# A two-layer hybrid encoder: the first two in-projection units by halves of the tokens, with all input tiles kept in SBUF and their squares behind the hi parts

## The chip, the core and the metric

The kernel runs on one core of one Trainium2 chip. The metric is the device time of one execution in microseconds, as the median of several runs. The engines that matter here are TensorE (PE in the profile), ScalarE (ACT), VectorE (DVE), GpSimd (POOL) and SyncE (SP), which only issues DMAs in this kernel.

## What is computed

Two layers over 1024 tokens of width 1024, in float32. Only the beginning of layer 0 is touched:

```python
def rms_norm(x, g, eps=EPS):
    xf = x.astype(jnp.float32)
    y = xf * lax.rsqrt(jnp.mean(xf * xf, axis=-1, keepdims=True) + eps)
    return (y * g.astype(jnp.float32)).astype(x.dtype)
...
h = rms_norm(x, norm_mix[0])
proj = h @ w_in                 # 1024 x 3328 columns: 26 units of 128
gate_b, gate_c, u = jnp.split(proj[..., :1536], 3, axis=-1)
y_a = gate_b * causal_depthwise_conv(gate_c * u, conv_w)
```

Behind it come the RWKV-7 mixer on the other 1792 columns, an output projection and a squared-ReLU MLP, then in layer 1 a sliding-window attention and a second MLP.

## The kernel before

**Layout.** The activations are kept with channels on the partitions and tokens on the free axis, as 8 chunks (k) of 128 channels by 1024 tokens. A float32 product is done as three: each operand is split into a high part in the reduced type fp32r (`h_hi`, `w_hi`, written by ACT) and the rest (`h_lo`, `w_lo`, written by DVE), and PE computes hi times hi, lo times hi and hi times lo. A unit is 128 columns of the weight: for each of 8 chunks three products, each for two halves of 512 tokens, 48 matmuls in all (`product`, L278), accumulated in two PSUM banks. Unit j uses weight slot j % 2 and banks 0 and 1, or 2 and 3.

**Input.** x comes with tokens on the partitions, in 8 tiles of 128 tokens by 1024 channels (512 KB), loaded by DMAs on POOL's queue (L1841) into `XIN`, which holds four; from the fifth on a load waits until the tile before it in that place is transposed and squared. PE transposes a tile by 8 matmuls with the identity (L1947) into two PSUM banks, taking banks 0 and 1 or 2 and 3 in turn, and ACT copies them into the residual `X` (L1901). DVE multiplies by the gain of the norm (L1992), ACT casts to `h_hi` (`x_high`, L1889), DVE subtracts to get `h_lo` (L1999). The products use x times gain without 1/rms, which is applied behind them, when a unit leaves PSUM. For 1/rms ACT squares the token-major tile with a row sum into `SSQ` (L1906), between its copy and its cast.

**1/rms.** ACT takes the root of the sums (L508, behind a table load), DVE the reciprocals (L516). PE spreads them over the partitions by 8 transposes into banks 4 and 5 (`spread` in `norm_between`, L546), inserted in unit 0 ahead of its chunk k = 5. ACT copies them to `RI` (`rms_spread`, L512). DVE's `scale_out` (L557) takes a unit out of PSUM, times `RI`, and frees its banks.

**Order.** PE waits for all eight tiles of `h_lo`, then does units 0 and 1 and 24 more in a loop. SP loads unit u into slot u % 2 once the low part of unit u - 2 is done (`load_unit`, L227). ACT casts it (`split_hi`, L233) once the unit that used the slot is through PE, DVE subtracts (`split_lo`, L237). For the first 12 units DVE's loop in `in_dve` is: low split of unit j + 1, wait for unit j, scale it out; after every third unit the convolution, five more operations (L822 to L831), whose result POOL stores with a DMA (L1844, `ya_spill`). Then `shift` does the token shift of each of the other 14 units.

Of the kernel before, what the change touches and what calls it, by code (L numbers as in the profile page):

```python
# [17 lines left out]
ACT = mybir.ActivationFunctionType  # L18
# [4 lines left out]
P = 128  # L23
D = 1024
S = 1024
KD = D // P
# [62 lines left out]
def hybrid_trunk(nc, x, norm_mix, norm_mlp, mlp_up, mlp_down, w_in_ab, conv_w, shift_mu, w0,  # L89
# [46 lines left out]
    RIV = at("rms_inverse_tokens", [2 * NT], 188.6875)  # L136
    XIN = at("x_in_tile", [4, KD, P], 120)
    VROW = at("vector_rows", [P], 136)

# [33 lines left out]
    with ExitStack() as ctx:  # L173
# [10 lines left out]
        ident_in, const_in, late_in = sem("ident_in"), sem("const_in"), sem("late_const_in")  # L184
        x_in = [sem(f"x_in{j}") for j in range(4)]
        lora_zero, dist_in = sem("lora_pads_zero"), sem("distances_in")
# [604 lines left out]
        def in_act(act):  # L791
            def splits(first, end):
                with act.Fori(first, end) as i:
                    for j in range(2):
                        split_hi(act, 1 - j, i + j, 2 * i + j + 2)

            splits(0, 7)
            act.wait_ge(shift_done, 2 + 2)
            nc.scalar.activation(WA[0:RH, :], WA[0:RH, :], ACT.Tanh).then_inc(lora_act, 1)
            nc.scalar.activation(GL[:, :], GL[:, :], ACT.Sigmoid).then_inc(lora_act, 1)  # L800
            splits(7, 12)
            split_hi(act, 1, 12, 26)

        def in_dve(dve):
# [4 lines left out]
            with dve.Fori(0, 2) as i:  # L809
                for q in range(2):  # L810
                    for r in range(3):
                        j = 3 * q + r
                        split_lo(dve, (j + 1) % 2, 6 * i + j + 1)
                        dve.wait_ge(acc_done, 6 * i + j + 3)
                        dve.wait_ge(conv_done, 2 * i + q + 1)
                        scale_out(dve, (ST0[:, 0:S], ST1[:, 0:S], WA[:, 0:S])[r], j % 2)
                    g = 2 * i + q
                    w = VT[:, bass.ds(V_CW + g, 1)], VT[:, bass.ds(V_CW + 4 + g, 1)], \
# [17 lines left out]
            dve.wait_ge(shift_zero, 2)  # L836
            split_lo(dve, 1, 13)
            dve.wait_ge(gl_free, 5)
# [928 lines left out]
        def x_banks(tile):  # L1767
            return PS[:, 2 * (tile % 2):2 * (tile % 2) + 2, :].rearrange("p b (k n) -> p (b k) n", n=P)

# [60 lines left out]
        def _(pool):  # L1830
# [6 lines left out]
            for tile in range(NT):  # L1837
                if tile >= 4:
                    pool.wait_ge(x_tr, 2 + tile - 3)
                    pool.wait_ge(x_sq, tile - 3)  # L1840
                pool.dma_start(XIN[:, tile % 4], xin[tile]).then_inc(x_in[tile % 4], 16)  # L1841
            for g in range(4):
# [49 lines left out]
        def _(act):  # L1892
# [5 lines left out]
            for tile in range(NT):  # L1898
                cols = slice(tile * P, tile * P + P)
                act.wait_ge(x_tr, tile + 3)  # L1900
                nc.scalar.copy(X[:, :, cols], x_banks(tile)).then_inc(x_ev, 1)  # L1901
                if tile == NT - 1:
                    x_high(act, tile)
                if tile:
                    act.wait_ge(x_sq, tile)
                nc.scalar.activation(ST0[:, 0:S], XIN[:, tile % 4], ACT.Square, accum_out=SSQ[:, tile:tile + 1])\  # L1906
                    .then_inc(x_sq, 1)
                if tile < NT - 1:
                    x_high(act, tile)
                if tile == NT - 3:  # L1910
                    split_hi(act, 0, 0, 1)
            act.wait_ge(eps_set, 2)
# [25 lines left out]
        def _(t):  # L1938
# [3 lines left out]
            t.wait_ge(ident_in, 16)  # L1942
            for tile in range(NT):
                t.wait_ge(x_in[tile % 4], 16 * (tile // 4) + 16)
                t.wait_ge(x_ev, tile + 1)
                for k in range(KD):
                    m = nc.tensor.transpose(x_banks(tile)[:, k], XIN[:, tile % 4, k], ident)  # L1947
                m.then_inc(x_tr, 1)
                if tile == 0:
                    t.wait_ge(const_in, 16 * N_EARLY)  # L1950
                    nc.tensor.transpose(PS[:, 7, 0:V_ROWS], VROW[0:V_ROWS, :], ident[0:V_ROWS, 0:V_ROWS])\
                        .then_inc(vec_t, 1)
            t.wait_ge(h_lo, NT)
            product(t, 0, 0, 0, 0, 8, P, 0, Hh, Hl, between=norm_between(t, "in"))
            product(t, 1, 1, 0, 1, 8, P, 0, Hh, Hl)
            with t.Fori(1, 13) as i:
# [15 lines left out]
        def _(dve):  # L1972
# [8 lines left out]
            dve.wait_ge(vec_t, 1)  # L1981
            nc.vector.tensor_copy(VT[:, 0:V_ROWS], PS[:, 7, 0:V_ROWS]).then_inc(vec_ok, 1)
            dve.wait_ge(vec_ok, 1)
# [3 lines left out]
            for tile in range(NT + 1):  # L1987
                if tile < NT:
                    dve.wait_ge(x_ev, tile + 3)
                    if tile >= 2:  # L1990
                        dve.wait_ge(h_lo, tile - 1)
                    nc.vector.tensor_tensor(GX[tile % 2], X[:, :, tile * P:tile * P + P], vb(V_MIX, KD),  # L1992
                                            ALU.mult).then_inc(x_gain, 1)
                if tile == NT - 1:
                    split_lo(dve, 0, 0)
                if tile:
                    dve.wait_ge(h_hi, tile)
                    cols = slice((tile - 1) * P, tile * P)
                    nc.vector.tensor_tensor(Hl[:, :, cols], GX[(tile - 1) % 2], Hh[:, :, cols].bitcast(F32),  # L1999
                                            ALU.subtract).then_inc(h_lo, 1)  # L2000
            rms_invert(dve, 0)
            in_dve(dve)
# [42 lines left out]
```

## Time and profile before

| | |
|---|---|
| median of three timed runs | 2477.88 us |
| lowest and highest | 2476.68, 2485.06 us |
| the profiled execution's own time | 2479.71 us |
| its span (first to last instruction) | 2477.9 us |
| granted TensorE clock, mean | 0.971 |

The times of the rows below count from the first instruction of the span. Busy time of PE is the modelled time of matmuls, which overlap, so two matmuls that start 0.23 us apart can each be shown as 0.39 long. The granted clock is a share of the full 2.4 GHz.

### The profile page before, as it was taken

Reading aid. Unit: us, or ns where it says so; the run is one execution under the profiler, and the core shown is the slowest. Engines: PE = TensorE matmul, PEld = TensorE weight load, DVE = VectorE, ACT = ScalarE, POOL = GpSimd, SP = SyncE. Lnnn points to the kernel's source line nnn. Section 1 sums busy time; section 2 is a strip of 40 time slices with the busy share of each in tenths; the row PEclk is TensorE's granted clock in tenths of the full one; section 3 lists DMA queues with packets and bytes.
Section 4 is the critical chain, followed back from the end, with each engine's and each line's share of the span. In section 5 each row is a group of like instructions: output and inputs, shape, how many; then the busy total and the mean of one; then the engine's idle time right before and its main releaser. Section 6 shows DMA issues by size and latency. Waiting matters only on the chain.

```text
span 2477.9 us, 41465 instructions
## 1 busy us (share of the span) xinstructions
PE 2352.4 (95%) x16338; PEld 1918.6 (77%) x16338; DVE 1429.0 (58%) x1990; ACT 786.9 (32%) x1258; POOL 424.1 (17%) x405
## 2 busy tenths in 40 slices
PE   6999979999899999999999799787999999999999
PEld 5888867877787888888888688445878888888887
DVE  3444467775427567656765633575265766567655
ACT  5111134543304223322333222464142233223323
POOL 0000011111141102111111600242411121112110
PEclk7999989997999999999999899899999999999999
DMA  3221100000111111111111111000111111111112
GB/s 114 68 82 51 43 9 3 3 4 32 33 49 43 51 58 45 51 51 59 47 46 59 38 52 34 9 1 18 42 43 58 54 42 51 59 51 45 48 60 85
DMA packets 166156, 110.85 MB, mean 45 GB/s; under 512 B 3598, under 2 KB 163684, under 8 KB 166052
## 3 DMA queue, kind: packets, MB, share of 16 engines
q1 hardware_dynamic: 163756, 100.39, 13.5%
q0 software_dynamic: 2240, 8.91, 1.1%
q8 instruction: 83, 1.36, 0.2%
q14 instruction: 21, 0.17, 0.0%
q10 hardware_dynamic: 56, 0.01, 0.0%
HBM read 102.49 MB, written 6.29 MB: 44 GB/s over the span
## 4 chain that ended last, share of the span: by engine, by line
PE 88%; DVE 6%; issue 2%; ACT 2%; POOL 2%; DMA 0%; SPq 0%; DVEq 0%; POOLq 0%; ACTq 0%
PE ps L278 36%; PE ps L383 23%; PE ps L376 13%; PE ps L938 2%; PE ps L960 1%; PE ps L1646 1%; DVE probs L1674 1%; DVE softmax_stats L1679 1%; PE ps L332 1%; PE ps L989 1%; PE ps L1460 1%; POOL stage L488 1%; POOL stage L491 1%; PE ps L1615 1%; PE ps L1120 1%
## 5 line engine op out<-in xcount | busy, mean ns | idle before, releaser
L233 ACT CAST w_hi<-w_raw 128x1024 fp32r<-128x1024 f32 x180 | 189.3, 1052 | 854.0 <-PE ps L278 628.7
L278 PE MATMUL ps<-h_hi,w_hi 128*128 128x512 f32 x1312 | 411.8, 395 | 31.3 <-DVE h_lo L522 17.5
L278 PE MATMUL ps<-h_lo,w_hi 128*128 128x512 f32 x1312 | 408.2, 393 | 0.0
L278 PE MATMUL ps<-h_hi,w_lo 128*128 128x512 f32 x1312 | 407.5, 392 | 0.0
L672 DVE TENSOR_TENSOR residual<-residual,ps 128x512 f32<-128x512 f32 x448 | 299.8, 686 | 165.8 <-PE ps L383 162.1
L278 PEld LDWEIGHTS ps<-h_hi,w_hi 128*128 128x128 f32 x1312 | 246.1, 190 | 85.1 <-issue 13.3
L278 PEld LDWEIGHTS ps<-h_lo,w_hi 128*128 128x128 f32 x1312 | 249.0, 190 | 52.7
L278 PEld LDWEIGHTS ps<-h_hi,w_lo 128*128 128x128 f32 x1312 | 248.7, 190 | 52.4
L237 DVE TENSOR_TENSOR w_lo<-w_raw,w_hi 128x1024 fp32r<-128x1024 f32 x180 | 222.3, 1235 | 33.8 <-ACT w_hi L233 33.7
L640 POOL TENSOR_TENSOR w_sums_raw<-w_raw 128x256 f32<-128x256 f32 x64 | 52.5, 820 | 1076.6 <-DMA w_raw<-in_mlp_down 656.9
L376 PE MATMUL ps<-h_hi,w_hi 128*128 128x512 f32 x512 | 199.2, 389 | 0.0
L376 PE MATMUL ps<-h_lo,w_hi 128*128 128x512 f32 x512 | 199.2, 389 | 0.0
L376 PE MATMUL ps<-h_hi,w_lo 128*128 128x512 f32 x512 | 199.2, 389 | 0.0
L654 DVE SCALAR_TENSOR_TENSOR stage<-ps,rms_inverse 128x1024 f32<-128x1024 f32 x32 | 39.2, 1225 | 213.1 <-PE ps L278 213.1
L383 PE MATMUL ps<-t_hi,w_sums_hi 128*128 128x512 f32 x384 | 150.0, 391 | 0.0
L383 PE MATMUL ps<-t_hi,w_sums_lo 128*128 128x512 f32 x384 | 149.7, 390 | 0.0
L383 PE MATMUL ps<-t_lo,w_sums_hi 128*128 128x512 f32 x384 | 149.6, 390 | 0.0
L580 ACT CAST w_sums_hi<-w_sums_raw 128x1024 fp32r<-128x1024 f32 x64 | 67.1, 1048 | 231.0 <-POOL w_sums_raw L646 231.0
L557 DVE TENSOR_TENSOR stage<-ps,rms_inverse 128x1024 f32<-128x1024 f32 x31 | 38.0, 1225 | 130.0 <-PE ps L278 127.9
L376 PEld LDWEIGHTS ps<-h_hi,w_lo 128*128 128x128 f32 x512 | 96.1, 188 | 19.9
L376 PEld LDWEIGHTS ps<-h_hi,w_hi 128*128 128x128 f32 x512 | 96.1, 188 | 19.9
L376 PEld LDWEIGHTS ps<-h_lo,w_hi 128*128 128x128 f32 x512 | 96.1, 188 | 19.9
(295 smaller groups left out, 3899.3 us busy)
## 6 DMA issues: line engine op xcount, KB each, us to landing
w_raw<-in_mlp_up SPq DMA_DIRECT2D x64, 512.0 KB, 4.0
w_raw<-in_mlp_down SPq DMA_DIRECT2D x64, 512.0 KB, 3.4
w_raw<-in_w_in_ab SPq DMA_DIRECT2D x26, 512.0 KB, 3.8
w_raw<-in_w_qkv SPq DMA_DIRECT2D x10, 512.0 KB, 4.0
x_in_tile<-in_x POOLq DMA_DIRECT2D x8, 512.0 KB, 4.1
w_raw<-in_w_out_ab SPq DMA_DIRECT2D x8, 512.0 KB, 3.7
w_raw<-in_w_o SPq DMA_DIRECT2D x8, 512.0 KB, 3.6
out<-out_chunk SPq DMA_DIRECT2D x8, 512.0 KB, 3.2
```

Source lines behind the costliest of these rows:

```text
L233: nc.scalar.copy(WH[:, slot], WR[:, slot]).then_inc(w_hi, 1)
L237: nc.vector.tensor_tensor(WL[:, slot], WR[:, slot], WH[:, slot].bitcast(F32), ALU.subtract).then_inc(w_lo, 1)
L278: m = nc.tensor.matmul(acc(a_slot, half), ww, xx[:, k, half * HALF:(half + 1) * HALF], start=first, stop=last)
L332: m = nc.tensor.matmul(acc(j, half), ww, xx[:, k, half * HALF:(half + 1) * HALF], start=first, stop=last, skip_group_check=True)
L376: m = nc.tensor.matmul(acc(slot, half), ww, xx[:, k, half * HALF:(half + 1) * HALF], start=first, stop=last)
L383: m = nc.tensor.matmul(PS[:, bank_n, :], ww[:, c], xx[:, c], start=new and c == 0 and ww is wh and xx is bh, stop=c == 1 and ww is wl, ski ...
L557: nc.vector.tensor_tensor(dst, acc2(slot), RI[:, :], ALU.mult).then_inc(acc_free[slot], 1)
L580: nc.scalar.copy(WSH[:, d % 2], WSR[:, d % 2]).then_inc(s_hi, 1)
L640: TT(raw[:, 0], a21, a22, ALU.add).then_inc(w_sum, 1)
L654: return nc.vector.scalar_tensor_tensor(dst, src, 0.0, scale, ALU.max, ALU.mult)
L672: dn_dve.done(TT(xk, xk, PS[:, bank_n, :], ALU.add), step)
L938: m = MM(block_bank(bank_n, 32)[quarter(q), h], left[quarter(q), h], right[quarter(q), h], start=True, stop=True)
```

## The change

- `XIN` holds all 8 tiles, so POOL issues the eight loads with no wait between them; the vector rows' buffer moves behind it.
- The transposes of the input use PSUM banks 4 to 7 instead of 0 to 3, and the transposed vector rows bank 3 instead of 7.
- On ACT the eight squares stand behind the last cast to `h_hi` instead of between copy and cast of each tile. The cast of tile t - 1 stands behind the copy of tile t. The high parts of weights 0 and 1 are made behind the casts of tiles 3 and 5.
- PE does units 0 and 1 by halves of the tokens: unit 0 for tokens 0 to 511, as soon as four tiles of `h_lo` and the first weight are there (tile 7 is transposed inside it, behind its first chunk), unit 1 for the same tokens, then, when all of `h_lo` is there, unit 0 and unit 1 for tokens 512 to 1023. The spread of 1/rms stands inside the last of the four, ahead of its chunk k = 1.
- On DVE the low splits of weights 0 and 1 are done inside the input loop, and in `in_dve` the low split of unit j + 2 stands behind the scale-out of unit j instead of the low split of unit j + 1 ahead of it.

```diff
-    XIN = at("x_in_tile", [4, KD, P], 120)
-    VROW = at("vector_rows", [P], 136)
+    XIN = at("x_in_tile", [NT, KD, P], 120)
+    VROW = at("vector_rows", [P], 152)
...
-            splits(0, 7)
+            split_hi(act, 0, 1, 3)
+            splits(1, 7)
...
                     for r in range(3):
                         j = 3 * q + r
-                        split_lo(dve, (j + 1) % 2, 6 * i + j + 1)
                         dve.wait_ge(acc_done, 6 * i + j + 3)
                         dve.wait_ge(conv_done, 2 * i + q + 1)
                         scale_out(dve, (ST0[:, 0:S], ST1[:, 0:S], WA[:, 0:S])[r], j % 2)
+                        split_lo(dve, j % 2, 6 * i + j + 2)
...
-            split_lo(dve, 1, 13)
             dve.wait_ge(gl_free, 5)
...
         def x_banks(tile):
-            return PS[:, 2 * (tile % 2):2 * (tile % 2) + 2, :].rearrange("p b (k n) -> p (b k) n", n=P)
+            return PS[:, 4 + 2 * (tile % 2):6 + 2 * (tile % 2), :].rearrange("p b (k n) -> p (b k) n", n=P)
...
             for tile in range(NT):
-                if tile >= 4:
-                    pool.wait_ge(x_tr, 2 + tile - 3)
-                    pool.wait_ge(x_sq, tile - 3)
-                pool.dma_start(XIN[:, tile % 4], xin[tile]).then_inc(x_in[tile % 4], 16)
+                pool.dma_start(XIN[:, tile], xin[tile]).then_inc(x_in[tile], 16)
...
                 nc.scalar.copy(X[:, :, cols], x_banks(tile)).then_inc(x_ev, 1)
-                if tile == NT - 1:
-                    x_high(act, tile)
+                if tile:
+                    x_high(act, tile - 1)
+                if tile in (4, 6):
+                    split_hi(act, tile // 2 - 2, 0, 2)
+            x_high(act, NT - 1)
+            for tile in range(NT):
                 if tile:
                     act.wait_ge(x_sq, tile)
-                nc.scalar.activation(ST0[:, 0:S], XIN[:, tile % 4], ACT.Square, accum_out=SSQ[:, tile:tile + 1])\
+                nc.scalar.activation(ST0[:, 0:S], XIN[:, tile], ACT.Square, accum_out=SSQ[:, tile:tile + 1])\
                     .then_inc(x_sq, 1)
-                if tile < NT - 1:
-                    x_high(act, tile)
-                if tile == NT - 3:
-                    split_hi(act, 0, 0, 1)
...
+            def x_transposes(tile):
+                t.wait_ge(x_in[tile], 16)
                 t.wait_ge(x_ev, tile + 1)
                 for k in range(KD):
-                    m = nc.tensor.transpose(x_banks(tile)[:, k], XIN[:, tile % 4, k], ident)
+                    m = nc.tensor.transpose(x_banks(tile)[:, k], XIN[:, tile, k], ident)
                 m.then_inc(x_tr, 1)
...
+            def first_units(j, half, between):
+                for k in range(KD):
+                    if k in between:
+                        between[k]()
+                    w_h, w_l = WH[:, j, k * P:k * P + P], WL[:, j, k * P:k * P + P]
+                    for ww, xx in ((w_h, Hh), (w_h, Hl), (w_l, Hh)):
+                        first, last = k == 0 and ww is w_h and xx is Hh, k == KD - 1 and ww is w_l
+                        m = nc.tensor.matmul(acc(j, half), ww, xx[:, k, half * HALF:(half + 1) * HALF],
+                                             start=first, stop=last)
+                if half:
+                    m.then_inc(acc_done, 1)
+
+            x_transposes(0)
+            t.wait_ge(const_in, 16 * N_EARLY)
+            nc.tensor.transpose(PS[:, 3, 0:V_ROWS], VROW[0:V_ROWS, :], ident[0:V_ROWS, 0:V_ROWS]).then_inc(vec_t, 1)
+            for tile in range(1, NT - 1):
+                x_transposes(tile)
+            t.wait_ge(w_lo, 3)
+            t.wait_ge(h_lo, 4)
+            first_units(0, 0, {1: lambda: x_transposes(NT - 1)})
+            t.wait_ge(w_lo, 4)
+            t.wait_ge(vec_ok, 1)
+            first_units(1, 0, {})
             t.wait_ge(h_lo, NT)
-            product(t, 0, 0, 0, 0, 8, P, 0, Hh, Hl, between=norm_between(t, "in"))
-            product(t, 1, 1, 0, 1, 8, P, 0, Hh, Hl)
+            first_units(0, 1, {})
+            first_units(1, 1, {1: norm_between(t, "in")[5]})
...
-                if tile == NT - 1:
-                    split_lo(dve, 0, 0)
...
+                if tile in (4, 7):
+                    split_lo(dve, tile // 7, tile // 7)
             rms_invert(dve, 0)
```

## Rows read from the trace of the kernel before

**Rows 1.** The page of the kernel before, its part 1: engine, busy us (share of the span), instructions.

```profile
PE 2352.4 (95%) x16338; PEld 1918.6 (77%) x16338; DVE 1429.0 (58%) x1990; ACT 786.9 (32%) x1258; POOL 424.1 (17%) x405
```

**Rows 2.** Waits of PE, 37 to 330 us: us in total, times, longest.

```profile
PE ps L278 <- DVE h_lo L1999: 10.1, 1, 10.1
PE ps L1037 <- ACT prep_t L1161: 4.1, 1, 4.1
```

**Rows 3.** The chain of waits, 0 to 60 us: start, us, what.

```profile
12.76 1.24 DVE stage L1992
14.01 1.05 ACT h_hi L1889
```

**Rows 4.** Timeline, input tiles: start, us, engine, line, operation, out<-in, count, idle before.

```profile
8.79 3.62 PE L1947 MATMUL ps<-constants,x_in_tile 128*128 128x128 f32 x16
...
9.51 1.23 DVE L1992 TENSOR_TENSOR stage<-residual,vectors 128x1024 f32<-128x1024 f32 x1
...
12.62 1.06 ACT L1906 ACTIVATE stage<-x_in_tile 128x1024 f32<-128x1024 f32 x1
...
12.87 1.07 PE L1947 MATMUL ps<-constants,x_in_tile 128*128 128x128 f32 x8 [0.46 <-ACT residual L1901]
13.58 0.19 ACT L1906 ACTIVATION_READ_ACCUMULATOR stage<-x_in_tile 128x1 f32 x1
...
14.96 1.01 ACT L1901 COPY residual<-ps 128x1024 f32<-128x1024 f32 x1
...
16.00 1.23 DVE L1992 TENSOR_TENSOR stage<-residual,vectors 128x1024 f32<-128x1024 f32 x1 [0.89 <-ACT residual L1901]
...
16.11 1.94 PE L1947 MATMUL ps<-constants,x_in_tile 128*128 128x128 f32 x8 [2.18 <-ACT residual L1901]
...
17.15 1.22 DVE L1999 TENSOR_TENSOR h_lo<-stage,h_hi 128x1024 fp32r<-128x1024 f32 x1
```

**Rows 5.** Timeline of DVE alone, 60 to 120 us.

```profile
63.34 1.23 DVE L557 TENSOR_TENSOR stage<-ps,rms_inverse 128x1024 f32<-128x1024 f32 x1 [8.43 <-PE ps L278]
...
74.21 1.23 DVE L557 TENSOR_TENSOR decay_aaa_in<-ps,rms_inverse 128x1024 f32<-128x1024 f32 x1 [8.52 <-PE ps L278]
75.47 1.23 DVE L822 TENSOR_TENSOR stage<-stage,decay_aaa_in 128x1024 f32<-128x1024 f32 x1
```

**Rows 6.** Timeline, from the last square to the end of unit 0.

```profile
36.37 0.19 ACT L1906 ACTIVATION_READ_ACCUMULATOR stage<-x_in_tile 128x1 f32 x1
...
37.88 1.22 PE L278 MATMUL ps<-h_hi,w_hi 128*128 128x512 f32 x2 [10.07 <-DVE h_lo L1999]
...
38.25 0.20 DVE L516 RECIPROCAL rms_inverse_tokens<-rms_inverse_tokens 128x8 f32<-128x8 f32 x1 [0.43 <-ACT rms_inverse_tokens L508]
...
47.27 1.03 PE L546 MATMUL ps<-constants,rms_inverse_tokens 128*128 128x128 f32 x8
...
48.35 1.02 ACT L512 COPY rms_inverse<-ps 128x1024 f32<-128x1024 f32 x1 [10.12 <-PE ps L546]
...
52.55 1.23 DVE L557 TENSOR_TENSOR stage<-ps,rms_inverse 128x1024 f32<-128x1024 f32 x1 [0.98 <-PE ps L278]
```

**Rows 7.** Lines L332 and L278: count, ns min/median/max, first and last start us.

```profile
L332 PE MATMUL ps<-h_hi,w_lo x32: 387/389/628, 634.9 to 676.7; 128*128 128x512 f32 x32
...
L278 PE MATMUL ps<-h_hi,w_lo x318: 389/389/389, 64.0 to 279.1; 128*128 128x512 f32 x159
```

**Rows 8.** Slices, PE alone: from:to, length, PE busy, granted clock, DMA share, GB/s.

```profile
15.00:16.00 1.00, 0.00 (x0) 0.95 0.79 98
...
43.00:44.00 1.00, 1.00 (x5) 0.90 0.00 0
```

**Rows 9.** DMA queues, 5 to 9 us: packets, MB, share; an issue: KB, us to landing.

```profile
q0 software_dynamic: 427, 1.55, 98.5%
q1 hardware_dynamic: 92, 0.04, 3.4%
...
w_raw<-in_w_in_ab SPq DMA_DIRECT2D x1, 512.0 KB, 7.4
```

More of the change, by code:

```diff
@@ L184, in hybrid_trunk @@
         ident_in, const_in, late_in = sem("ident_in"), sem("const_in"), sem("late_const_in")
-        x_in = [sem(f"x_in{j}") for j in range(4)]
+        x_in = [sem(f"x_in{j}") for j in range(NT)]
         lora_zero, dist_in = sem("lora_pads_zero"), sem("distances_in")
@@ L1942, in _ @@
             t.wait_ge(ident_in, 16)
-            for tile in range(NT):
-                t.wait_ge(x_in[tile % 4], 16 * (tile // 4) + 16)
+            def x_transposes(tile):
+                t.wait_ge(x_in[tile], 16)
                 t.wait_ge(x_ev, tile + 1)
                 for k in range(KD):
-                    m = nc.tensor.transpose(x_banks(tile)[:, k], XIN[:, tile % 4, k], ident)
+                    m = nc.tensor.transpose(x_banks(tile)[:, k], XIN[:, tile, k], ident)
                 m.then_inc(x_tr, 1)
[L1949 to L1952, printed above, removed]
+            def first_units(j, half, between):
[20 more added lines that the diff above has]
+            first_units(1, 0, {})
             t.wait_ge(h_lo, NT)
-            product(t, 0, 0, 0, 0, 8, P, 0, Hh, Hl, between=norm_between(t, "in"))
-            product(t, 1, 1, 0, 1, 8, P, 0, Hh, Hl)
+            first_units(0, 1, {})
+            first_units(1, 1, {1: norm_between(t, "in")[5]})
             with t.Fori(1, 13) as i:
@@ L1981, in _ @@
             dve.wait_ge(vec_t, 1)
-            nc.vector.tensor_copy(VT[:, 0:V_ROWS], PS[:, 7, 0:V_ROWS]).then_inc(vec_ok, 1)
+            nc.vector.tensor_copy(VT[:, 0:V_ROWS], PS[:, 3, 0:V_ROWS]).then_inc(vec_ok, 1)
             dve.wait_ge(vec_ok, 1)
```

## The prediction

> **What bounds the kernel now.** First the page [rows 1]: TensorE (PE) is busy for 95% of the span, so almost every microsecond that is not a matmul is a wait of PE, and what matters is where these waits are. The view of waits, for PE alone and from 37 us to the end of the in-projection [rows 2], shows two: 10.1 us before the first product, until the last `h_lo` tile is there, and 4.1 us at the start of the next stage, behind the shifts of the last units. Between them 26 units run with no gap, one each 10.87 us. So the kernel pays for the time to the first product, 37.88 us, and then for PE's work. The chain of waits [rows 3] says what that time is: DVE gain, ACT cast, ACT copy, and round again, one tile of 128 tokens each 3.24 us (gains at 12.76 and 16.00 [rows 3, 4]). The timeline [rows 4] shows why: ACT does four things per tile, copy 1.01, square 1.06 and 0.19, cast 1.05, and they follow one another without a gap. DVE has only two operations of 1.23 and PE 1.07 to 1.94 of transposes.
>
> **When the first product can start after the change.** The squares leave ACT's loop, so a tile costs ACT two instructions, 2.0 us. DVE becomes the slower one: gain(t), then h_lo(t-1), 1.15 from start to start (16.00 to 17.15 [rows 4]), then gain(t+1), which waits for DVE's own h_lo(t-1) to be complete; such a dependent pair is 1.26 from start to start (74.21 to 75.47 [rows 5]). That makes 2.41 us a tile. Gain(0) stays at 9.51 [rows 4]. Tile 1 is transposed in half of the group of 16 (3.62 us from 8.79 [rows 4]), by 10.6, and is copied 10.7 to 11.7; gain(1) 11.75, h_lo(0) 12.9, gain(2) 14.16, gain(4) two tiles on at 18.98, h_lo(3) 20.13, the first weight's low part 21.28, done at 22.50 (a split is the same operation as h_lo, 1.22 [rows 4]). Its high part is made on ACT behind the cast of tile 3 (17.85 to 18.9), by 19.9, inside DVE's time: nothing. Tile 6 is transposed behind the copy of tile 4 (done 17.4), by 19.4. So the half products start at 22.6 instead of 37.88, **15.3 us earlier**.
>
> **What PE does from there.** Units end where DVE's scale-outs start: unit 0 by 52.55, unit 1 by 63.34, unit 2 by 74.21 [rows 5, 6], the later ones 10.87 apart. Now there are four half units of 24 matmuls, as many as two whole units, and one weight load for each matmul in both forms. Another place already works by halves (L332): the median of its matmuls is 389 ns, as is that of L278 in the body of the in-projection [rows 7]. No extra. Added inside is only tile 7's transposes. They last 1.94 at the low clock [rows 4], but lie in a stretch that is low anyway: the clock was low, 1.2 GHz, from the first product to about 43.2 (the granted share is 0.90 in the slice from 43 [rows 8], so a fifth of it at one half), 5.3 us after PE began. I take the same 5.3 us from 22.6 on. Eight transposes at full clock are 1.07, at the low one 1.94, and what they put off from the low stretch runs fast, so they cost **1.0**. The spread of `RI` (1.03 [rows 6]) is in both. Before, two units took 37.88 to 63.34, 25.5 us. After: 22.6 + 25.5 + 1.0 = 49.1, against 63.34.
> The four parts separately: first units 0 half 0 to 31.7 (three matmuls and the transposes to 25.9, then five more at 0.45, twice the 0.2265 that 10.87 / 48 gives for one at the full clock, then 16 at 0.2265), unit 1 half 0 to 37.1, unit 0 half 1 to 42.5, unit 1 half 1 with the spread to 49.0, which agrees with the 49.1 above. Sum: 15.3 - 1.0 = **14.3 us earlier** at unit 2.
>
> **Covers, and what each costs if it goes.** *Second weight:* DVE goes on with gain(5) 22.5, h_lo(4), gain(6) 24.9, h_lo(5), gain(7) 27.3, h_lo(6) 28.4, second low part 29.6 to 30.8, last h_lo to 31.9. PE wants the second weight at 31.7 (0.9 to spare) and the last h_lo at 37.1 (5 to spare). *Squares:* they stand behind the last cast, ACT 29.5 to 38.9 (eight of 1.15, 12.62 to 13.77 [rows 4], and 0.03 for each one's wait on the one before). Table load, root and reciprocal take 1.9 more (36.56 to 38.45 [rows 6]), 40.9. PE wants the reciprocals after the first k of the last half, at 43.2: 2.3 to spare, and beyond that each microsecond costs one. *Scales and unit 2:* the spread now comes after unit 0, so unit 0's scale-out waits for `RI`, ACT's cast of weight 2 stands behind the `RI` copy, and DVE's split behind the scale-out. From the spread's start to the copy 1.08 (47.27 to 48.35 [rows 6]), copy 1.02, scale-out 1.15 to the next start, split 1.22: 4.5 us, ready at 47.7, while PE needs it at 49.0 (21 matmuls and the spread are 5.8). 1.3 to spare, whatever the clock does before it.
> *Low splits in the loop:* split of unit j+2 behind scale-out j is the old order shifted, except that at every third unit it stands ahead of the convolution's five operations instead of behind them. ACT's cast for it runs beside the scale-out, so it delays the convolution by 1.2 us and takes 1.2 from its end; DVE idles 8.5 us before such a unit and PE is never short there [rows 2, 5]. The SP queue's loads of those units are released earlier, not later. The `ya_spill` stores on POOL's queue start 1.2 us later; DVE's scale-out of unit 12 waits for the last of them, and PE needs that bank only a unit later. Nothing.
> *Loads:* POOL issues the last four input tiles at once instead of at 10.7 to 20.8, beside the small vector rows and SP's two weights. In the slice 5 to 9 us the POOL queue had 98.5% of the engines' time and moved 1.55 MB, SP's 3.4% [rows 9], so I let all input go first: eight tiles of 0.52 MB at 0.39 MB/us are 10.8 us, from about 4 to about 15, all before PE's turn at tiles 5 to 7. Weight 0 landed 7.4 after its issue, at 11.8, with four tiles ahead [rows 9]; four tiles more are 5.4 us, so 17.2. It is wanted on ACT at 18.9 and DVE stands still only if it lands after 20.2. Nothing, and if weights share with tiles, sooner.
>
> **The sum.** The profiled execution took 2479.7 with a span of 2477.9; median of the three timed runs 2477.88. The span would be 2463.6, that execution's own time 2465.4, the median **2463.6 us**. Behind unit 2 everything hangs on PE or on chains that start with it, so I carry all 14.3 to the end.
>
> **Clock and transposes.** Tile 3's eight transposes took 1.07 [rows 4], as the spread's eight at full clock, 1.03 [rows 6], and PE had run nothing but transposes; the eight of tile 4, after a pause of 2.2 us, took 1.94 and the granted clock had fallen at 15.9 (a granted share of 0.95 in the slice from 15 [rows 8]). The Trainium skill (TensorE: Matmul & The Clock Gate, Part 4: PE-mode transpose) says that the full clock doesn't engage for transposes. By that rule tile 3 should have been slow; the trace speaks against it.
>
> **Rivals.**
> A. *DVE's loop doesn't speed up* (it stays at a tile each 3.24 us, for a wait that I don't see). Then h_lo(3) ends as before, near 24.9, the split at 26.1, and the gain is 37.88 - 26.1 - 1.0 = 10.8: 2467.1. For it: three engines in turn hand the tile on. Against: the PSUM pairs let ACT copy a tile ahead. 0.07. This is the lower bound of the gain.
> B. *Transposes don't count toward the clock's rise.* The low stretch from 22.6 lasts 1.94 longer, costing half of it: 2464.6. The skill's rule above is of this kind. Against: tile 3. 0.10.
> C. *The clock is still up at 22.6.* It last fell 2.0 us after PE stopped; here the pause is 3 us or more, so it should have fallen, but one fall is thin evidence. Unit 0 half 0 would end at 29.2 and PE would wait for the second weight, 30.8: gain 0.8 more, 2462.8. 0.15.
> D. *The reciprocals are late.* Squares or root take over 2.3 us longer, PE stands at the spread: 1 to 3 us lost, 2465 to 2467. Against: ACT has nothing else to do then. 0.06.
> E. *Absorbed.* A later stage is paced by something that didn't move (a load, DVE's backlog), and the time stays near 2478. For it: the 4.1 us at the stage border. Against: that wait is DVE's shifts of the last unit, which start when PE ends it. 0.04.
> F. *Slower: the first weight starves behind eight input tiles.* Place: ACT's cast of weight 0, with copies 5 to 7 queued behind it. PE then starts 2.3 after the landing; it eats the gain from a landing at 34.5 on, and is slower by over 0.3% from 42. For it: 3.4% of the engines for SP while tiles moved. Against: the tiles are through by 15. 0.02.
> Mine: 0.56.
>
> **Range and chances.** 0.3% of the time, 7.4 us, is about what a measurement of this kernel can tell from no change, so faster means under 2470.4. My case with A to D gives 2462.8 to 2467.1. The timed runs reach from 1.2 below their median to 7.2 above it, and later stages with a changing clock may shift a microsecond or two either way: 2460.0 to 2468.5. Faster 0.94 (mine, A to D), same 0.04 (E), slower 0.02 (F).
>
> **What the changed profile would show.** First half product near 22.6 (over 25: A, or the landing of weight 0); DVE gains 2.4 apart; squares on ACT from about 29.5 to 39; PE's clock low to about 28; no wait of PE at the spread (else D); unit 2 from about 49; every later stage 14 us earlier. The forecast is wrong if PE waits anew between 31 and 49, or if the stages behind don't move with it.

## The result, and the profile after

The changed kernel took 2462.23 us (median of six runs, 2456.04 to 2471.02), the kernel before in the same rounds 2477.28 (2475.13 to 2488.42). The ratio is 0.9922, with a 95% interval of 0.9892 to 0.9951: faster by more than 0.3%. The median lies in the predicted range, 1.4 us from the forecast. The ratio times the 2477.88 shown before is 2458.6, and that lies 1.4 us below the range. Two executions in a slower state, one of each kernel, are left out of the ratios and means of this document; with them the difference of the means given further down, 17.4 us, would be 16.5.

The profiled execution of the changed kernel has a span of 2469.2 us, only 8.7 less than that of before. Its front answers to the prediction within a few tenths. First the timeline of the changed kernel, the first tile's transposes, tiles 2 and 3, the first half product, and what follows to unit 2 (start, us, engine, line, operation):

```profile
5.87 1.94 PE L1944 MATMUL ps<-constants,x_in_tile 128*128 128x128 f32 x8 [5.87 <-DMA x_in_tile<-in_x]
...
14.33 1.23 DVE L2009 TENSOR_TENSOR stage<-residual,vectors 128x1024 f32<-128x1024 f32 x1
15.47 1.22 DVE L2014 TENSOR_TENSOR h_lo<-stage,h_hi 128x1024 fp32r<-128x1024 f32 x1
...
16.79 1.22 DVE L2009 TENSOR_TENSOR stage<-residual,vectors 128x1024 f32<-128x1024 f32 x1
...
17.69 1.06 PE L1944 MATMUL ps<-constants,x_in_tile 128*128 128x128 f32 x8 [0.94 <-ACT residual L1898]
...
22.80 0.80 PE L1954 MATMUL ps<-h_hi,w_hi 128*128 128x512 f32 x1 [4.04 <-DVE w_lo L237]
...
29.80 1.06 ACT L1907 ACTIVATE stage<-x_in_tile 128x1024 f32<-128x1024 f32 x1
...
39.04 0.18 ACT L1907 ACTIVATION_READ_ACCUMULATOR stage<-x_in_tile 128x1 f32 x1
...
40.93 0.20 DVE L516 RECIPROCAL rms_inverse_tokens<-rms_inverse_tokens 128x8 f32<-128x8 f32 x1 [8.71 <-ACT rms_inverse_tokens L508]
...
43.00 1.03 PE L546 MATMUL ps<-constants,rms_inverse_tokens 128*128 128x128 f32 x8
```

```profile
45.48 1.22 DVE L557 TENSOR_TENSOR stage<-ps,rms_inverse 128x1024 f32<-128x1024 f32 x1 [4.34 <-ACT rms_inverse L512]
46.62 1.22 DVE L237 TENSOR_TENSOR w_lo<-w_raw,w_hi 128x1024 fp32r<-128x1024 f32 x1
48.86 1.22 DVE L557 TENSOR_TENSOR stage<-ps,rms_inverse 128x1024 f32<-128x1024 f32 x1 [1.02 <-PE ps L1954]
```

The gains stand 2.46 us apart (14.33 to 16.79) where they stood 3.24 apart [rows 3, 4]. The first half product starts at 22.80 instead of 37.88 [rows 6]. The squares run from 29.80 to 39.22, the reciprocals are done at 41.13, and PE comes for them at 43.00 without a wait. Unit 1 ends at 48.86 instead of 63.34 [rows 5]. The second fence is DVE's timeline: unit 0's scale-out at 45.48, split of weight 2 done at 47.84, 0.8 us before PE wants it (unit 2's first matmul starts at 48.66).

The waits of PE from 20 to 330 us in the changed kernel, which answer to [rows 2] (us in total, times, longest):

```profile
PE ps L1037 <- ACT prep_t L1161: 4.1, 1, 4.1
PE ps L1954 <- DVE w_lo L237: 4.0, 1, 4.0
PE ps L1116 <- POOL prep_t L1417: 4.0, 1, 4.0
```

The 10.1 us are gone; what PE still waits for is the first weight's low part, from 18.8 to 22.8. The 4.1 at the stage border is the same; the third row belongs to the next stage, which now reaches into this window. The in-projection is over, and the RWKV stage's first matmul (L996) starts, at 309.9 us instead of 324.3, in the view of that line:

```profile
L996 PE MATMUL ps<-decay_aaa_in,lora_w x64: 271/272/579, 309.9 to 549.4; 64*128 64x128 f32 x64
```

So 14.4 us were given where the change is, against 14.3 forecast, and 5.7 of them are not in this execution's span. They go in the stage behind it. Slices of the changed kernel, PE alone (from:to, length, PE busy, granted clock, DMA share, GB/s):

```profile
18.00:22.00 4.00, 0.76 (x7) 0.83 0.00 1
27.00:28.00 1.00, 1.00 (x5) 0.78 0.00 0
309.90:581.70 271.80, 246.12 (x6153) 0.90 0.03 10
490.00:492.00 2.00, 1.37 (x20) 0.91 0.04 8
492.00:515.00 23.00, 22.95 (x225) 0.50 0.01 2
```

The third line is the RWKV stage, from its first matmul to its last `bonus` product on DVE (L1387): 271.8 us at a granted clock of 0.90. Its counterpart in the kernel before:

```profile
324.30:590.80 266.50, 240.51 (x6153) 0.92 0.03 10
```

That is 5.3 us shorter. In the changed kernel's execution PE runs at half clock, 1.2 GHz, for some 24 us from about 491.6 on, in the middle of that stage, although it is busy all the while. Whether that is the change's doing or chance is what the first experiments ask.

### The profile page after: what moved, and what is told of

Its sections match the earlier page's. It is cut to its first block, busy times and chain, and to the rows that moved or that the text cites. A ratio compares the mean times of both kernels' runs of the same rounds, so it can differ in the third digit from the quotient of the medians.

```text
span 2469.2 us, 41455 instructions
## 1 busy us (share of the span) xinstructions
PE 2355.8 (95%) x16338; PEld 1922.5 (78%) x16338; DVE 1429.8 (58%) x1990; ACT 787.2 (32%) x1258; POOL 424.3 (17%) x405
## 3 DMA queue, kind: packets, MB, share of 16 engines
q1 hardware_dynamic: 163756, 100.39, 13.6%
## 4 chain that ended last, share of the span: by engine, by line
PE 89%; DVE 5%; issue 2%; POOL 2%; ACT 1%; DMA 0%; SPq 0%; DVEq 0%; POOLq 0%; ACTq 0%
PE ps L278 36%; PE ps L383 23%; PE ps L376 13%; PE ps L938 2%; PE ps L960 1%; PE ps L1646 1%; DVE probs L1674 1%; PE ps L1954 1%; PE ps L332 1%; DVE softmax_stats L1679 1%; PE ps L989 1%; PE ps L1615 1%; POOL stage L488 1%; PE ps L1460 1%; PE ps L1120 1%
## 5 line engine op out<-in xcount | busy, mean ns | idle before, releaser
L278 PE MATMUL ps<-h_hi,w_hi 128*128 128x512 f32 x1280 | 400.2, 394 | 21.4 <-DVE h_lo L522 17.7
L278 PE MATMUL ps<-h_lo,w_hi 128*128 128x512 f32 x1280 | 397.1, 392 | 0.0
L278 PE MATMUL ps<-h_hi,w_lo 128*128 128x512 f32 x1280 | 396.1, 391 | 0.0
L278 PEld LDWEIGHTS ps<-h_hi,w_hi 128*128 128x128 f32 x1280 | 239.3, 189 | 73.2 <-issue 13.6
L278 PEld LDWEIGHTS ps<-h_lo,w_hi 128*128 128x128 f32 x1280 | 241.9, 189 | 51.2
L278 PEld LDWEIGHTS ps<-h_hi,w_lo 128*128 128x128 f32 x1280 | 241.7, 189 | 50.9
L376 PE MATMUL ps<-h_hi,w_lo 128*128 128x512 f32 x512 | 199.2, 389 | 0.0
L376 PE MATMUL ps<-h_hi,w_hi 128*128 128x512 f32 x512 | 199.2, 389 | 0.0
L376 PE MATMUL ps<-h_lo,w_hi 128*128 128x512 f32 x512 | 199.2, 389 | 0.0
L376 PEld LDWEIGHTS ps<-h_hi,w_lo 128*128 128x128 f32 x512 | 96.1, 188 | 20.0
L376 PEld LDWEIGHTS ps<-h_lo,w_hi 128*128 128x128 f32 x512 | 96.1, 188 | 19.9
L376 PEld LDWEIGHTS ps<-h_hi,w_hi 128*128 128x128 f32 x512 | 96.1, 188 | 19.9
```

Of the source, the lines that this page charges most:

```text
L278: m = nc.tensor.matmul(acc(a_slot, half), ww, xx[:, k, half * HALF:(half + 1) * HALF], start=first, stop=last)
L376: m = nc.tensor.matmul(acc(slot, half), ww, xx[:, k, half * HALF:(half + 1) * HALF], start=first, stop=last)
```

## The experiments

In all of them L996's first start tells what the in-projection took, L1387's last start where the RWKV stage ends, both from the views of those lines.

**The two kernels again.** No edit.

> The changed kernel unaltered. In its first profile the RWKV stage's first matmul (L996) starts at 309.9 us against 324.3 before, so the in-projection gives 14.4, yet the spans differ by 8.7 only, because of the stage from there to the last `bonus` product (L1387): 271.8 us against 266.5. Theory 1: the in-projection's 14.4 is the whole effect, and the 5 us that the stage takes more are the TensorE clock, which falls there at a moment that differs from one execution to the next. Then L996 starts at 309.9 again within 0.5, that stage's length is another one, between 262 and 275, and goes with the time spent at the low clock, and the timed ratio is about 0.994. Theory 2: the change itself makes that stage slower or faster (another start, another order of loads). Then the stage takes 271.8 again within 1 us.

> The kernel before, unaltered, as the measure of what two sets of runs of one kernel differ by. Theory 1 (later stages vary with the clock): L996 starts at 324.3 within 0.5, the stage from there to the last L1387 takes another length than 266.5, within 262 to 275, and the ratio's interval holds 1.000, with an interval about as wide as that of the changed kernel, 0.3%. Theory 2 (the change alters the stage): 266.5 again within 1 us.

Measured: changed kernel 2462.54 (nine runs, 2451.21 to 2474.50), ratio 0.9924 (0.9892 to 0.9955); kernel before against itself 0.9984 (0.9951 to 1.0017). L996 started at 309.8 and 324.8. The changed kernel's RWKV stage took 264.1 this time, 7.7 less than in its first profile, and that of the kernel before 264.3:

```profile
309.80:573.90 264.10, 238.68 (x6181) 0.94 0.03 8
```

Matmuls that were slow in the first profile (first fence, changed kernel, 16 of line L1120 in 3.51 us, 188 us into the stage) take 1.89 in this one at the same point of the stage (second fence, 186 us into it):

```profile
497.84 3.51 PE L1120 MATMUL ps<-token_major,nt_rk 128*128 128x64 f32 x16
```

```profile
496.19 1.89 PE L1120 MATMUL ps<-token_major,nt_rk 128*128 128x64 f32 x16
```

Theory 1 holds: one program, another length of the stage. Of the 5.7 us that the first profile lacked, 5.3 lie in this stage, and they were the clock's.

**Whole units.** Everything as changed, but the two first units whole.

```diff
-            for tile in range(1, NT - 1):
+            for tile in range(1, NT):
                 x_transposes(tile)
-            t.wait_ge(w_lo, 3)
-            t.wait_ge(h_lo, 4)
-            first_units(0, 0, {1: lambda: x_transposes(NT - 1)})
-            t.wait_ge(w_lo, 4)
-            t.wait_ge(vec_ok, 1)
-            first_units(1, 0, {})
             t.wait_ge(h_lo, NT)
-            first_units(0, 1, {})
-            first_units(1, 1, {1: norm_between(t, "in")[5]})
+            product(t, 0, 0, 0, 0, 8, P, 0, Hh, Hl, between=norm_between(t, "in"))
+            product(t, 1, 1, 0, 1, 8, P, 0, Hh, Hl)
```

> The changed kernel with units 0 and 1 whole again, after all eight tiles, the spread ahead of chunk 5 of unit 0; input tiles, squares and splits stay as changed. Theory 1 (the halves give what the profile shows): all of `h_lo` is there at 32.2 us as in the changed kernel, the first product starts at 32.3, units 0 and 1 take the 25.5 us that they took before, so unit 1 ends at 57.8: 5.5 earlier than before and 8.9 later than changed, about 2471. Rival (halves gain little, since PE's first microseconds run at the low clock anyway, and moving the squares did most): unit 1 ends within 3 us of the changed kernel's 48.9.

The timeline of this kernel:

```profile
32.33 1.22 PE L278 MATMUL ps<-h_hi,w_hi 128*128 128x512 f32 x2 [10.12 <-DVE h_lo L2008]
...
57.37 1.23 DVE L557 TENSOR_TENSOR stage<-ps,rms_inverse 128x1024 f32<-128x1024 f32 x1 [8.43 <-PE ps L278]
```

First product at 32.33 and unit 1 done at 57.37, as the first theory had it (32.3, 57.8); L996 at 318.4. Everything but the halves (squares behind, casts and splits moved, eight places for tiles) is thus worth 5.9 us at that mark, and the halves 8.5. But the timed ratio, 0.9927 (0.9899 to 0.9955), was that of the changed kernel. It was run again:

> The changed kernel unaltered, to narrow the mean. So far one straight line fits all 100 timed executions of five kernels: span = a level of the kernel + 0.40 us for each us of low granted clock, with 2.2 us left over. If the later stages vary with the clock alone, L996 starts at 309.9, the RWKV stage's length falls on the line through the ten profiles so far (about 250 us + 0.48 per us at low clock), and the mean span stays near 2460.5. If the change alters a later stage, the stage falls off that line by more than 3 us.

> The kernel with whole units again, beside after_third on one chip. Its mean span was only 2.6 us above the changed kernel's, where the marks in the profiles say 8.5 (L996 at 318.4 against 309.9). If that was chance of the clock, L996 starts at 318.4 again and the mean over both sets of runs moves towards 2469; at equal low time it stays 5 above the changed kernel. If the halves lose later what they give in the in-projection, the mean stays within 3 us of the changed kernel's at an equal share of low clock in the later stages.

Measured: whole units 2472.83 (twelve runs), ratio 0.9970 (0.9941 to 0.9999), L996 at 318.2; changed kernel 2459.74 (six runs), ratio 0.9896 (0.9852 to 0.9941), L996 at 310.6. The changed kernel's mark is 0.7 later than expected: the low clock of its front lasted to 28.9 in this execution, against 27.4 in the first profile, and unit 1 ended at 49.62 instead of 48.86. Over all timed executions the mean span is 2459.7 for the changed kernel (20), 2469.4 for whole units (20) and 2477.1 for the kernel before (73). The first set was chance: whole units stand 9.6 above the changed kernel, standard error 2.7, where the marks say 8.5. The clock says so too: the executions of whole units had 115 us of low clock on average in the first set and 138 in the second, those of the changed kernel 115 to 121 in its three sets (worked out as in the table further down, over the whole span). At an equal total of low clock whole units are 5.7 above the changed kernel (standard error 0.7; 5 was expected). Their front holds 13.6 us of low clock against 6.8, so at an equal amount in the later stages it is 8.5, by the price of 0.41 that is worked out below.

**Squares inside the loop.**

```diff
                 if tile in (4, 6):
                     split_hi(act, tile // 2 - 2, 0, 2)
-            x_high(act, NT - 1)
-            for tile in range(NT):
                 if tile:
                     act.wait_ge(x_sq, tile)
                 nc.scalar.activation(ST0[:, 0:S], XIN[:, tile], ACT.Square, accum_out=SSQ[:, tile:tile + 1])\
                     .then_inc(x_sq, 1)
+            x_high(act, NT - 1)
```

> The changed kernel with each square back in ACT's loop, behind the cast of the tile before; halves, eight input buffers and splits stay. Theory 1 (ACT's four operations per tile were the pace, the squares' place sets it): tiles 3.2 us apart again, first half product near 25.5 instead of 22.8, and the second weight's low part near 36, so PE waits for it behind the first half; unit 1 ends near 53, 4 later than changed, about 2466. Rival (the hand-over between three engines is the pace, not ACT's work): tiles stay 2.4 apart and unit 1 ends at 49.

Tiles were 2.9 us apart (DVE's gains at 14.85, 17.74 and 20.64), not 3.2; the first half product started at 24.19 instead of 22.80, and PE waited again before the second unit's half:

```profile
34.77 0.80 PE L1953 MATMUL ps<-h_hi,w_hi 128*128 128x512 f32 x1 [2.25 <-DVE w_lo L237]
```

At the end of that wait, at about 34.6, the granted clock fell (0.65 in the slice from 34 to 36, 0.50 in the next, 1.00 from 38). Unit 1 ended at 53.84, 5.0 later than changed, L996 at 314.9; ratio 0.9949 (0.9923 to 0.9975), ten runs. The first theory holds in kind, since ACT's square costs the loop 0.44 us a tile. That the loop is quicker than in the kernel before with the same four instructions is read from the two timelines: here ACT goes from one to the next without a wait, while before each cast waited 0.24 us for its own tile's gain. The other PSUM banks and the eight places for tiles are in this kernel too, and no run separates them.

**The spread one half unit sooner.**

```diff
-            first_units(0, 1, {})
-            first_units(1, 1, {1: norm_between(t, "in")[5]})
+            first_units(0, 1, {1: norm_between(t, "in")[5]})
+            first_units(1, 1, {})
```

> The changed kernel with the spread of 1/rms ahead of chunk 1 of unit 0's second half instead of unit 1's. PE comes there at about 37.6 us, while in the changed kernel the reciprocals are done at 41.1. Theory (what stands behind the squares is counted rightly, and PE waits for it one for one): PE stands for 3.5 us ahead of the spread, unit 1 ends at 52.4 instead of 48.9, and L996 starts at 313.4 instead of 309.9. Rival (the order squares, table load, root, reciprocals has slack elsewhere, or the wait is taken up again before the end of the in-projection): L996 below 312. The time itself can't tell 3.5 us.

The waits of PE, 15 to 305 us, and a slice at the place:

```profile
PE ps L1954 <- DVE w_lo L237: 4.1, 1, 4.1
PE ps L546 <- DVE rms_inverse_tokens L516: 2.8, 1, 2.8
```

```profile
44.00:46.00 2.00, 2.00 (x6) 0.50 0.00 0
```

PE stood 2.8 us for the reciprocals (it came later than assumed, the clock having risen at 29.0 in this execution). Then the clock, which had been full, fell at 42.7 and stayed low to 46.1. Unit 1 ended at 54.27 and L996 came at 315.3. The low clock of the front ended at 29.0 here, as in after_third (28.9), whose unit 1 ended at 49.62 and whose L996 came at 310.6. Against that execution it is 4.7 later for a wait of 2.8, and the rest is close to half of the 3.4 us of low clock behind it; against the first profile (309.9) it is 5.4, of which 0.7 are the place of the first low stretch. So the reciprocals stood where they were counted, and a wait there is dearer than one for one, as it was in squares_inside. One execution, 2469.12 us.

**Convolution first.** At r = 2 the low split goes behind the five operations again.

```diff
                         scale_out(dve, (ST0[:, 0:S], ST1[:, 0:S], WA[:, 0:S])[r], j % 2)
-                        split_lo(dve, j % 2, 6 * i + j + 2)
+                        if r < 2:
+                            split_lo(dve, j % 2, 6 * i + j + 2)
...
                     nc.vector.tensor_tensor(GL[:, :], GL[:, :], ST0[:, 0:S], ALU.mult).then_inc(conv_done, 1)
+                    split_lo(dve, q % 2, 6 * i + 3 * q + 4)
```

> The changed kernel with the low split at each third unit behind the convolution's five operations, as in the kernel before, instead of ahead of them. Theory (nothing there is on PE's path in either order): no wait of PE in the in-projection, L996 starts at 309.9 within 0.3. Rival (the earlier split is part of the gain): L996 later than 310.5.

L996's counterpart came at 309.6, and behind unit 1 PE had no wait in the in-projection: the place of these splits is worth nothing. One execution, 2461.29 us. It shows something else, ahead of the edit's place. The low clock lasted only from 22.2 to 25.6 here, PE was through with the first half sooner, and it stood 0.36 us for the second weight:

```profile
31.07 0.50 PE L1956 MATMUL ps<-h_hi,w_hi 128*128 128x512 f32 x1 [0.36 <-DVE w_lo L237]
```

**Transposes and split sooner.**

```diff
-            for tile in range(1, NT - 1):
+            for tile in range(1, NT):
                 x_transposes(tile)
...
-            first_units(0, 0, {1: lambda: x_transposes(NT - 1)})
+            first_units(0, 0, {})
...
-                if tile in (4, 7):
-                    split_lo(dve, tile // 7, tile // 7)
+                if tile in (4, 6):
+                    split_lo(dve, tile // 5, tile // 5)
```

> The changed kernel with tile 7's transposes ahead of the half products, where PE waits for the first weight's low part (18.8 to 22.8 us), and the second weight's low part one tile sooner on DVE. Theory: first half product at 22.8 as before; no transposes inside; unit 0 half 0 ends at about 30.4 instead of 31.4 and the second weight is there at 28.6. The last gain and so the squares come 1.1 later, the reciprocals at 42.2, where PE arrives for the spread at 41.9. Unit 1 ends near 47.9 instead of 48.9, L996 at 308.9. The time would be 1 us less, which the runs can't tell from none; the marks in the profile can. Rival (what is taken out is lost to the later reciprocals or the second weight): unit 1 at 48.7 or later.

Unit 1 ended at 48.81 and L996 came at 309.8, no sooner than changed. The rival's number, but for another reason: PE's arrival for the reciprocals was not too early. The low clock lasted from 22.3 to 29.1 in this execution, against 20.6 to 27.4 in the changed kernel's (0.83 in the slice from 18 to 22, 0.78 in that from 27), so PE had 6.2 us at half clock from its first product on instead of 4.6, which ate what was saved:

```profile
22.00:24.00 2.00, 1.35 (x6) 0.56 0.00 0
28.00:30.00 2.00, 2.00 (x7) 0.73 0.01 4
```

The later place of the low stretch isn't the edit's doing: the unaltered changed kernel had it from 22.1 to 28.9 in after_third, with unit 1 done at 49.62 and L996 at 310.6. Against that execution split_sooner is 0.8 sooner at both marks, nearly the 1.0 that was forecast. One execution of each is thin evidence, but the term is not shown to be nothing.

Ratio 0.9935 (0.9907 to 0.9963), ten runs: not told apart from the changed kernel.

**Fillers.** On top of that, transposes of the identity while PE waits.

```diff
+            def fill(n):
+                for _ in range(n):
+                    nc.tensor.transpose(PS[:, 2, 0:P], ident, ident)
+
             for tile in range(1, NT - 1):
                 x_transposes(tile)
+            fill(14)
+            x_transposes(NT - 1)
+            fill(5)
```

> As split_sooner, and PE does 14 transposes of the identity, whose results nobody reads, ahead of tile 7's transposes and 5 behind them, so that it transposes nearly without a pause from 8.9 to 22.8 us. Theory 1 (transposes hold the TensorE clock up as matmuls do): the granted clock doesn't fall at 20.6, unit 0 half 0 takes 5.4 us at full clock and ends at 28.3, PE waits 0.3 for the second weight and about 2 for the reciprocals, so unit 1 ends at 47.9 all the same. Theory 2 (transposes don't count for the clock): it falls at about 20.6 or sooner and unit 0 half 0 ends at 30.4.

Slices of this kernel:

```profile
309.10:604.70 295.60, 265.97 (x6182) 0.84 0.03 8
18.00:20.00 2.00, 2.00 (x21) 1.00 0.01 3
20.00:22.00 2.00, 1.18 (x12) 1.00 0.00 0
22.00:24.00 2.00, 1.91 (x13) 1.00 0.04 8
```

and PE's spread in its timeline:

```profile
42.20 1.09 PE L546 MATMUL ps<-constants,rms_inverse_tokens 128*128 128x128 f32 x8 [1.60 <-DVE rms_inverse_tokens L516]
```

The clock stayed at 1.00 from the transposes into the products, which ran at 0.23 us from the second on; in every other execution it fell before the first product. PE then waited 1.6 us for the reciprocals, and unit 1 ended at 48.12, L996 came at 309.1. The first theory holds on the clock and, within 0.2, on the end. Beyond it, the RWKV stage of this one execution took 295.6 us at 0.84, the longest of all, for 2485.00 us in total; nothing of the front reaches there.

**What the clock costs over all runs.** For each profiled execution, the length of the RWKV stage and the time in it at the low clock, which is 2 x (1 - granted share) x length (shares are given to 0.01, so within 3 us):

```
execution        L996   stage  low      execution        L996   stage  low
squares_inside   314.9  257.3  15       after            309.9  271.8  54
conv_first       309.6  263.8  26       whole_again      318.2  271.9  49
after_again      309.8  264.1  32       spread_early     315.3  272.7  55
before_again     324.8  264.3  32       split_sooner     309.8  275.9  61
before           324.3  266.5  43       whole_units      318.4  281.6  73
                                        fillers          309.1  295.6  95
```

A straight line through these and after_third (287.4, 80), 249.1 + 0.46 x low, misses none by more than 2.7 us, whichever kernel it is. Over the 133 timed executions of five kernels, fitted with one slope and a level for each, a microsecond of low clock costs 0.41 us and 2.3 us are left over. At an equal total of low clock the changed kernel is 6.7 us below the kernel before (standard error 0.6). Its front holds 6.8 us of low clock (20.6 to 27.4) where the other's holds 27.3 (15.9 to 43.2), so at an equal amount in the later stages the difference is 6.7 + 0.41 x 20.5 = 15.0. (It takes the front's low clock as the same in every execution of a kernel; it was 6.8 in all three profiles of the changed kernel and 27.3 in both of the kernel before, but 3.4 in conv_first, whose front is that of the changed kernel.)

## Why the prediction was right, and where it was not

- *The pace of the input tiles.* Forecast 2.41 us with DVE as the limit, measured 2.46; the dependent pair was 1.32 instead of 1.26. First half product forecast 22.6, measured 22.80. Rival A is out. What set the pace before was misread, though. The prediction has ACT's four operations follow one another without a gap; in the kernel before each cast waited for its own tile's gain (timeline of ACT):

```profile
17.26 1.05 ACT L1889 CAST h_hi<-stage 128x1024 fp32r<-128x1024 f32 x1 [0.24 <-DVE stage L1992]
```

The pace of 3.24 was the round of copy, gain and cast of one tile (starts at 14.96, 16.00, 17.26 and the next copy at 18.21), and the square ran beside the gain. Estimated from these rows, taking the square out of the old order would have saved nothing; no run had that. The cast's new place, behind the next tile's copy, opened the round: of the 0.78 us saved a tile 0.34 came with it (squares_inside), and the square was worth the other 0.44 only then. The prediction had counted both changes but given the reason to the square alone.
- *PE from there.* Forecast 5.3 us of low clock and 1.0 for tile 7's transposes, unit 1 done at 49.1; measured 4.6 and 48.86. The 4.6 is partly luck: from first product to rise it was 2.8 in conv_first and 6.0 in after_third, and the place of that rise moved unit 1's end by 0.8 (48.86, 49.62) in one and the same program, as much as the whole term of 1.0 for the transposes.
- *Covers.* Second weight 31.08 against PE's 31.44 (0.4 to spare, not 0.9), reciprocals 41.13 against 43.00 (1.9, not 2.3), split of weight 2 at 47.84 against 48.66 (0.8, not 1.3). In the first profile none was used up; in conv_first, with the clock up earlier, the first was, by 0.36. Spread_early took the second away, and its price was 4.7 for 2.8 at an equal place of the first low stretch, so "each microsecond costs one" was too cheap. The low splits in the loop cost nothing (conv_first).
- *Loads.* Weight 0 landed 12.6 us after its issue at 4.38, at 17.0, forecast 17.2. It was wanted at 19.0. Rival F had no ground. The number was right for another reason than the one given: the input didn't all go first, but from 9 to 15 us both queues moved as many packets each, and the weights' are small (last section). The tiles went on to between 15 and 16.
- *Transposes and clock.* Rival B is out: tile 0's eight transposes took 1.94 us at 5.87, tile 6's eight took 1.06 at 17.69, and PE did nothing but transposes in between, so the clock rose with them. (The recorded share reads 1.00 from the start, before any rise; this one is read from the durations.) Fillers shows that they also hold it. The rule in the Trainium skill (TensorE: Matmul & The Clock Gate, Part 4: PE-mode transpose), that the full clock doesn't engage for them, is not what this chip did, as these two rows of the changed kernel show. With longer pauses they didn't raise it: in the kernel before, the eight of each tile took 1.94 us in every 3.25 from 16.11 on, and the clock stayed low. C did not happen, the clock fell at 20.6, and in no other execution of that front was it still up at the first product, though it fell as late as 22.2.
- *The carry to the end.* The 14.4 us of the in-projection reach the end in the mean: 2477.1 - 2459.7 = 17.4, standard error 2.1, or 15.0 at an equal clock. The other 2.4 are some 6 us less of low clock in the later stages of the changed kernel's executions, no more than chance gives. D and E did not happen.
- *What failed* is one step, the range's allowance: "later stages with a changing clock may shift a microsecond or two either way". Between executions of one program the RWKV stage alone moved from 264.1 to 271.8 (changed kernel) and from 271.9 to 281.6 (whole units), and over kernels that differ only ahead of it from 257.3 to 295.6, where the term allowed one or two. Timed executions of the kernel before spread with a standard deviation of 8.3 us (spans from 2459.3 to 2498.4, 73 of them). A median of six then has a standard error of some 4 us, estimated as 1.25 x 8.3 / square root of 6, and the difference of two such some 6. So it is luck that the median of six lay 1.4 us from the forecast, and as much luck that the ratio's 19.3 us (2477.88 less 2458.6) lay 5 us beyond the 14.3; the better measure of the gain is the 14.4 at the mark. The range needed about 14.3 plus or minus 7, an estimate. The trace of the kernel before gave a sign of it: the RWKV stage stood at a granted clock of 0.92, and nothing said that it would be so in the next execution.

What is still open: why the clock falls where it does in the RWKV stage. The runs show that it differs between executions of one program and what it costs, not what sets the moment. Fillers in that stage weren't tried.

## What to carry to other kernels

A front of a kernel in which PE waits for all of its input can be cut by letting the first units run on the part that is there, and by shortening the loop that prepares the input; here the two gave 8.5 and 5.9 us of 324. In such a loop look first for the round between engines: an operation that runs beside another engine's work costs nothing until the round is opened (here by the cast standing one tile later), and only then is it worth taking out. When a mark in the profile can be placed just behind the change (here L996's first start, steady to 0.8 us between executions of one program), read the gain there, since end-to-end times that spread by 8 us can't tell 14 from 20, nor 8 from nothing in one set of rounds. Before a range is given, look for stages that run at a mixed granted clock: their length is a matter of chance, and its price is some 0.4 us for each microsecond at half clock.

## What the runs showed of the hardware

- The RWKV stage, the same in all these kernels, has between 15 and 95 us at half clock, though PE is busy for nine tenths of it. More than half of its matmuls are 32x32; that this is why the clock falls is not shown.
- A wait of PE of 2.8 us, some 40 us into the kernel, was followed by 3.4 us of low clock. In the changed kernel's front the clock fell at 20.2, 20.6 or 22.1 in three executions with the same work, PE having stopped at 18.8 each time. Transposes of the identity in that wait, 14 in 1.69 us and 5 in 0.71, kept the clock up.
- The two DMA queues, while both moved data, shared by packets and not by bytes. Queues of the changed kernel from 9 to 12 us (packets, MB, share of 16 engines):

```profile
q0 software_dynamic: 288, 1.05, 86.9%
q1 hardware_dynamic: 290, 0.15, 16.5%
```

From 12 to 15 us it was 283 and 283 packets. Input tiles come in packets of about 3.6 KB, weights of 0.5 KB, and with as many packets each the weights got a seventh of the bytes that the tiles got.
